# Norm passages of a three-block kernel: rows scaled first and turned by transposes, lower parts in one step, a new order of steps

## The reference, cut to what matters

```
def rmsnorm(x, g):                       # also rms_norm, rmsnorm_3
    return x * lax.rsqrt(jnp.mean(x * x, axis=-1, keepdims=True) + EPS) * g

# end of the first block
x = x + rmsnorm(mix, norm_post)          # mix = concat(...) @ w_out
# second block: begins and ends
h = rms_norm(x, norm_g);  proj = h @ w_in
...
x = x + y @ w_out
x = rms_norm(x, final_g)
# third block: begins
h = rmsnorm_3(h_res, ln_g) * (1.0 + scale[:, None]) + shift[:, None]
p = h @ w_in + b_in
```

## Time and profile before

| | us |
|---|---|
| median of three runs | 2825.24 |
| lowest, highest | 2823.49, 2826.43 |
| the profiled execution, device time | 2824.86 |
| its span on the profile page | 2823.0 |

### The profile page before, as it was taken

One profiled execution on the slowest core, in us unless ns is written; L12 is line 12 of the kernel. 1 busy time (PEld: TensorE's weight loads), 2 busy tenths in 40 slices (PEclk: granted clock), 3 DMA queues, 4 the chain that ended last, 5 costly groups with the idle time before them and its releaser, 6 DMA issues.

```text
span 2823.0 us, 38380 instructions
## 1 busy us (share of the span) xinstructions
PE 2793.6 (99%) x15512; PEld 2333.6 (83%) x15512; DVE 1409.7 (50%) x2509; ACT 1073.7 (38%) x1818; POOL 365.3 (13%) x627
## 2 busy tenths in 40 slices
PE   8999999999999999999999999999999999999998
PEld 7888777888899888888888889887777777788888
DVE  6686644436327544554554236335544453545534
ACT  5332234454226333322222236434443444333322
POOL 6457154100001000000000001000000000000011
PEclk9999999999999999999999999999999999999999
DMA  7567465324326444566664335542222223232423
GB/s 203 146 184 125 123 146 123 105 82 164 109 90 193 153 149 149 153 186 183 186 179 151 140 97 134 123 97 68 71 68 72 68 68 97 75 83 82 149 97 120
DMA packets 449153, 352.52 MB, mean 125 GB/s; under 512 B 73869, under 2 KB 404461, under 8 KB 444753
## 3 DMA queue, kind: packets, MB, share of 16 engines
q1 hardware_dynamic: 412818, 241.93, 30.6%
q0 software_dynamic: 36160, 108.14, 13.0%
HBM read 322.81 MB, written 22.81 MB: 122 GB/s over the span
## 4 chain that ended last, share of the span: by engine, by line
PE 95%; DVE 3%; DMA 1%; ACT 1%; issue 0%; POOL 0%; SPq 0%; DVEq 0%; ACTq 0%
PE bank L3615 57%; PE bank L3655 16%; PE bank L3625 4%; PE bank L3678 2%; PE bank L3573 2%; PE bank L2381 1%; PE bank L2432 1%; PE bank L2408 1%; PE bank L667 1%; DMA ring<-in_w_in 1%; PE bank L2502 1%; PE bank L2454 1%; PE bank L730 1%; DVE ring_parts L3768 1%; PE bank L694 0%; PE bank L663 0%
## 5 line engine op out<-in xcount | busy, mean ns | idle before, releaser
L3768 DVE TENSOR_TENSOR ring_parts<-ring,ring_hi 128x1024 fp32r<-128x1024 f32 x420 | 510.4, 1227 | 724.9 <-ACT ring_hi L3727 720.4
L3727 ACT ACTIVATE ring_hi<-ring 128x1024 fp32r<-128x1024 f32 (+1 forms) x424 | 441.3, 1051 | 599.9 <-DMA ring<-in_w_in 300.3
L3615 PE MATMUL bank<-A_parts,ring_hi 128*128 128x512 f32 x1552 | 618.2, 398 | 2.0 <-DVE ring_parts L3768 2.0
L3615 PE MATMUL bank<-A_parts,ring_parts 128*128 128x512 f32 x1552 | 605.6, 390 | 0.0
L3615 PE MATMUL bank<-X_parts,ring_hi 128*128 128x512 f32 x1360 | 529.6, 389 | 0.0
L3615 PE MATMUL bank<-B_parts,ring_hi 128*128 128x512 f32 x1224 | 478.8, 391 | 0.0
L3615 PEld LDWEIGHTS bank<-A_parts,ring_hi 128*128 128x128 f32 x1552 | 291.6, 188 | 66.7 <-issue 8.8
L3615 PEld LDWEIGHTS bank<-A_parts,ring_parts 128*128 128x128 f32 x1552 | 291.3, 188 | 62.5
L3615 PEld LDWEIGHTS bank<-X_parts,ring_hi 128*128 128x128 f32 x1360 | 255.6, 188 | 50.8
L3615 PE MATMUL bank<-B_parts,ring_parts 128*128 128x512 f32 x752 | 292.7, 389 | 0.0
L3615 PEld LDWEIGHTS bank<-B_parts,ring_hi 128*128 128x128 f32 x1224 | 230.0, 188 | 51.8 <-issue 5.1
(11 more groups left out here) (573 smaller groups left out, 3904.6 us busy)
## 6 DMA issues: line engine op xcount, KB each, us to landing
ring<-in_w_in SPq DMA_DIRECT2D x288, 512.0 KB, 3.8
ring<-in_w_out SPq DMA_DIRECT2D x96, 512.0 KB, 3.6
work<-in_w_ada POOLq DMA_DIRECT2D x96, 512.0 KB, 4.8
ring<-in_w_in SPq DMA_DIRECT2D x48, 256.0 KB, 3.8
ring<-in_w_mem_kv SPq DMA_DIRECT2D x16, 512.0 KB, 4.1
x_keep<-X POOLq DMA_DIRECT2D x8, 1024.0 KB, 4.8
X<-x_keep POOLq DMA_DIRECT2D x8, 1024.0 KB, 10.2
X<-in_x SPq DMA_DIRECT2D x4, 1024.0 KB, 10.9
```

What stands on the lines that cost most here:

```text
L3615: mm = nc.tensor.matmul(K.ps(st)[0:w + (t["beside"] or 0), 0:t["n"]], lhsT=wp[:, j, :], rhs=columns(ap, kk), start=first, stop=end)
L3727: nc.scalar.activation(slot_view[key](ring_hi), slot_view[key](ring), ACT.Copy).then_inc(s_hi, 1)
L3768: nc.vector.tensor_tensor(lo, slot_view[key](ring), slot_view[key](ring_hi), ALU.subtract).then_inc(s_lo, 1)
```

## The change

It does the following, and nothing outside the two passages:

- `d` makes the reciprocal and then scales the row tile itself by VectorE, in two halves of 1024 columns, into a buffer of its own (`K.scaled_rows`: in `K.work`, four buffers in passage one, two that are used in turn in passage two, where `d` of tiles 2 and 3 first waits that the tile two before is turned). In passage two both factors are applied in one instruction. PE waits for each half by itself.
- `T` turns the scaled rows by `nc.tensor.transpose` with the identity.
- In passage one `G` writes the rounded `h_hi` at once, and no longer waits for the store of `X`. `P` is, for each bank, four `scalar_tensor_tensor` of 128x128 that read the bank, multiply by the gain and subtract `h_hi`, giving `h_lo`; it waits for the store of `X`. Passage two keeps its `G` and `P`.
- `F` of passage two no longer waits for PE.
- Both orders in `LAST_COLUMNS` are new. In passage two F1, F2 and F3 now stand behind P31, and in passage one T00 ahead of W30.

```diff
--- before.py
+++ after.py
@@ -26,12 +26,12 @@
 
 
 LAST_COLUMNS = {
-    2: """W00 W10 W01 W11 E0 V0 M0 S0 R0 F0 W20 E1 V1 Q0 M1 W21 S1 m0 R1 s0 F1 W30 E2 d0 Q1 V2 M2 T00 S2 m1 R2 s1 F2 G00 W31
-          P00 a00 Q2 T01 d1 E3 m2 b00 G01 V3 T10 M3 P01 G10 T11 P10 s2 G11 d2 P11 T20 S3 a01 a10 T21 a11 R3 b01 F3 H00 b10 Q3
-          b11 m3 s3 G20 d3 P20 T30 G21 P21 T31 G30 H10 P30 G31 P31 H01 H11""",
-    3: """W00 W10 W01 W11 V0 E0 Z0 M0 S0 R0 m0 W20 V1 s0 E1 d0 Z1 M1 S1 R1 m1 T00 s1 d1 G00 T10 P00 T01 G10 W21 F0 G01 P10 W30
-          P01 V2 W31 E2 Z2 M2 S2 R2 m2 a00 T11 V3 s2 E3 d2 G11 M3 b00 T20 P11 T21 S3 a01 a10 b01 F1 F2 a11 H00 Z3 R3 b10 G20
-          m3 b11 s3 G21 d3 P20 T30 G30 P21 T31 P30 H10 G31 F3 P31 H01 H11""",
+    2: """W00 W10 W01 E0 M0 V0 S0 R0 W11 W20 E1 F0 M1 V1 S1 Q0 R1 F1 m0 s0 Q1 d0 m1 W21 E2 M2 T00 W30 V2 S2 R2 G00 s1 W31
+          F2 Q2 E3 T01 d1 P00 G01 V3 m2 T10 s2 M3 P01 T11 S3 a00 G10 d2 R3 b00 T20 a01 F3 a10 b01 P10 G11 Q3 P11 T21 m3 s3
+          H00 G20 b10 a11 d3 P20 T30 G21 T31 G30 b11 G31 P21 P30 H10 P31 H01 H11""",
+    3: """W00 W10 W01 V0 E0 Z0 M0 W11 S0 R0 m0 s0 V1 Z1 W20 d0 E1 T00 M1 W21 S1 R1 m1 s1 G00 d1 T10 P00 V2 G10 T01 E2 P10
+          G01 Z2 M2 W30 F0 S2 T11 W31 P01 a00 G11 R2 a01 V3 b00 E3 m2 P11 Z3 M3 s2 d2 a10 T20 S3 R3 G20 b01 b10 m3 T21 a11
+          H00 s3 P20 d3 T30 G21 G30 b11 P21 P30 T31 G31 H10 P31 F1 H01 F2 F3 H11""",
     None: """W00 W10 W01 W11 V0 E0 M0 S0 R0 F0 W20 V1 E1 M1 S1 R1 F1 W21 W30 V2 E2 M2 S2 R2 F2 W31 V3 E3 M3 S3 R3 F3"""}
 PROJ_BANKS = (0, 1, 2)
 PAIR_BANKS = (0, 1)
@@ -1430,16 +1430,26 @@
     x_keep = nc.dram_tensor("x_keep_2", (SEQ, D), F32).ap()
     s_keep = [K.sem(f"x_rows{tt}_kept_2") for tt in range(TT)]
     s_back = K.sem("x_back_2")
-    h_whole = K.X.rearrange("p t (k c) -> p t k c", c=P)
 
     def norm_parts(k4, tt):
         four = slice(4 * k4, 4 * k4 + 4)
-        return h_hi[:, four, tt * P:(tt + 1) * P], h_whole[:, tt, four, :], h_lo[:, tt, four, :]
-
-    def norm_gain_wait(act, tt):
-        act.wait_ge(s_par, K.par_count[2])
-        act.wait_ge(s_keep[tt], 16)
-    K.norm_parts[2], K.norm_gain_wait[2] = norm_parts, norm_gain_wait
+        hi = h_hi[:, four, tt * P:(tt + 1) * P]
+        return hi, hi, h_lo[:, tt, four, :]
+    K.norm_parts[2] = norm_parts
+    K.norm_gain_wait[2] = lambda act, tt: act.wait_ge(s_par, K.par_count[2])
+
+    def norm_lo(vec, src, k4):
+        tt = src[2]
+        if k4 == 0:
+            vec.wait_ge(s_keep[tt], 16)
+        vec.wait_ge(*bk.half_released(src, k4))
+        hi, _, lo = norm_parts(k4, tt)
+        for j in range(4):
+            kk = 4 * k4 + j
+            ins = nc.vector.scalar_tensor_tensor(lo[:, j, :], ps(src, k4)[:, j * P:(j + 1) * P], norm_g[:, kk:kk + 1], hi[:, j, :],
+                                                 ALU.mult, ALU.subtract)
+        ins.then_inc(bk.free_sem(src, k4), 1)
+    K.norm_lo[2] = norm_lo
     a = K.arena()
     v = a("b2_v", 2, TT, GLA_VD)
     r = a("b2_r", 2, 2, NC)
@@ -1828,7 +1838,6 @@
 
     def vec_final(vec, L, st):
         tt = st[2]
-        vec.wait_ge(*bk.filled(("norm", 3, tt), KT // 4 - 1))
         nc.vector.tensor_scalar(X[:, tt, :], X[:, tt, :], K.rstd_out[:, tt:tt + 1], None, ALU.mult).then_inc(K.x_done, 1)
 
     K.sq_junk[2] = K.hn[:, 1, :].rearrange("p (a c) -> p a c", c=NC)
@@ -3098,6 +3107,7 @@
         self.slot_src, self.slot_count, self.slot_used = {}, {"wo": 8}, {}
         self.const_loads, self.wait_gain, self.par_at = [], {}, 0
         self.sp_start, self.mix_parts, self.norm_parts, self.norm_gain_wait = [], {}, {}, {}
+        self.norm_lo = {}
         self.sq_junk, self.wo_releases = {}, {}
         self.act_wo_row, self.vec_wo_row, self.split_at = {}, {}, {}
         self.act_row_square, self.act_row_square_2, self.square_no, self.paired_tiles = {}, {}, {}, {}
@@ -3180,7 +3190,8 @@
         K.blocks, K.modulated = list(blocks), False
         K.par = K.sb("par", PAR)
         K.hn = K.work[:, 0:2 * D].rearrange("p (a d) -> p a d", d=D)
-        K.row_scale = {nxt: K.work[:, at:at + TT * P].rearrange("p (t c) -> p t c", c=P) for nxt, at in ((2, 6 * D), (3, 3 * D))}
+        K.scaled_rows = {2: lambda tt: K.work[:, tt * D:(tt + 1) * D],
+                         3: lambda tt: K.work[:, (3 * D, 6 * D + P)[tt % 2]:(3 * D, 6 * D + P)[tt % 2] + D]}
         K.sq = K.sb("square_sums", TT, SUMS)
         K.sq_2 = K.work[:, 4 * D:4 * D + TT * SUMS].rearrange("p (t n) -> p t n", n=SUMS)
         K.out_squared = K.work[:, 4 * D + TT * SUMS:4 * D + TT * SUMS + TT]
@@ -3275,11 +3286,15 @@
             nc.vector.reciprocal(r, r).then_inc(s_brstd, 1)
             vec.wait_ge(s_brstd, recip_no[st] + 1)
             if kind == "in_scale":
-                scale = K.row_scale[blk][:, tt, :]
-                if blk == 2:
-                    nc.vector.tensor_scalar(scale, K.ident[:, :], r, None, ALU.mult).then_inc(s_hn, 1)
-                else:
-                    nc.vector.tensor_scalar(scale, K.ident[:, :], r, out, ALU.mult, ALU.mult).then_inc(s_hn, 1)
+                if blk == 3 and tt >= 2:
+                    vec.wait_ge(*bk.filled(("norm", 3, tt - 2), KT // 4 - 1))
+                for half in range(2):
+                    cols = slice(half * D // 2, (half + 1) * D // 2)
+                    rows = K.scaled_rows[blk](tt)[:, cols]
+                    if blk == 2:
+                        nc.vector.tensor_scalar(rows, X[:, tt, cols], r, None, ALU.mult).then_inc(s_hn, 1)
+                    else:
+                        nc.vector.tensor_scalar(rows, X[:, tt, cols], r, out, ALU.mult, ALU.mult).then_inc(s_hn, 1)
 
 
         block_of = BLOCKS
@@ -3539,14 +3554,13 @@
                 if st[0] == "norm":
                     _, blk, tt, half = st
                     st = st[0:3]
-                    if half == 0:
-                        pe.wait_ge(s_hn, scaled_no["in_scale", blk, tt] + 1)
+                    pe.wait_ge(s_hn, 2 * scaled_no["in_scale", blk, tt] + half + 1)
+                    rows = K.scaled_rows[blk](tt)
                     for k4 in (2 * half, 2 * half + 1):
                         bk.take(pe, st, k4)
                         for j in range(4):
                             kk = 4 * k4 + j
-                            mm = nc.tensor.matmul(K.ps(st, k4)[:, j * P:(j + 1) * P], lhsT=X[:, tt, kk * P:(kk + 1) * P],
-                                                  rhs=K.row_scale[st[1]][:, tt, :], start=True, stop=True)
+                            mm = nc.tensor.transpose(K.ps(st, k4)[:, j * P:(j + 1) * P], rows[:, kk * P:(kk + 1) * P], K.ident[:, :])
                         mm.then_inc(bk.full_sem(st, k4), 1)
                 elif st[0] == "pair":
                     _, st, pair = st
@@ -3756,6 +3770,9 @@
                     if tt == 0 and h == 0:
                         K.wait_gain[blk](vec)
                     for k4 in (2 * h, 2 * h + 1):
+                        if blk in K.norm_lo:
+                            K.norm_lo[blk](vec, src, k4)
+                            continue
                         hi, whole, lo = K.norm_parts[blk](k4, tt)
                         vec.wait_ge(*bk.half_released(src, k4))
                         L(nc.vector.tensor_copy(hi, whole))
```

## The result

The changed kernel takes 2834.56 us (median of 7 runs, 2833.78 to 2835.74), the kernel before 2825.24 (7 runs, 2823.32 to 2828.09): ratio 1.0035, 95% interval 1.0026 to 1.0044. It is slower by 9.3 us; forecast were 6. The profiled execution took 2834.19 us, its span is 2832.4.

The account below looks back on a forecast made before the run. The prediction took both passages as ties between PE and the pair ACT and DVE, PE's savings kept only if P31 comes earlier. Its terms, 0.7 + 0.8 + 3.7 + 0.8 = +6.0 us, gave 2831, range 2822 to 2838.

Parts of the forecast that it names:

- Turns: PE time in both passages: transposes at 0.11 us instead of 0.23 save 14.7 us; bounds 0 and 14.7.
- Scaling: DVE time per row tile: 1.33 against 0.20 us in passage one, 1.46 against 0.25 in passage two.
- Lower parts: Subtractions of passage one on DVE: 1.05 us a bank against 1.06 before, neither gain nor loss; bounds -4 to +5 us.
- Passage one: P31 of passage one ends 0.7 us later and PE gives back all of its 7.4 us; bounds -0.5 to +4.
- the clock: PE's granted clock falls in idle times: +0.8 us in passage one, +0.8 behind passage two; bounds 0 and 3.2.
- Passage two: P31 comes 0.6 us earlier, PE stands idle some 8 us ahead of T20; bounds -1.2 and +1.5.
- The stores: Behind P31 of passage two: last store of x issued near 1749.8, 5.3 us later than before, landing at 1758.
- Behind the landing: From the last store's landing to the next tile 3.6 us: it starts at 1761.6, +3.7 us; bounds +0.2 and +8.3.
- the clock falls and the loads starve: Rival, chance 0.12: three clock falls at 1.6 us, stores landing at 1762.6, split slots late as well: +12 us, 2837.

Follow-up runs that it names:

- f_pool: The changed kernel with F0 to F3 of passage two on POOL, each as soon as its tile's halves are scaled: 2839.49 us, ratio 1.0053.
- turned_first: The changed kernel with the buffer `turned` moved to tile 0 of X, its writer waiting for that store alone: 2830.29 us, ratio 1.0020.
- f_ahead: The changed kernel with F1 to F3 of passage two ahead of P31 again: 2827.28 us, ratio 1.0008.

## Why the prediction came out as it did

The direction, the place of the loss and its mechanism (late stores, met by the weight loads, release the evacuation of `gates`) were right. The size was too small: the time of 2834.6 lies in the range, 3.6 us above the 2831 forecast, and it came that near in part by luck. Step by step:

- **Turns**: 0.11 us and a factor of two, as said; PE keeps nothing of it. Right. Timeline of PE and DVE, answering to the earlier trace rows:

```profile
881.87 1.91 PE L3563 MATMUL bank<-ident,work 128*128 128x128 f32 x16
```
```profile
860.46 1.42 DVE L3295 TENSOR_SCALAR work<-X,rstd 128x1024 f32<-128x1024 f32 x2
861.79 2.15 DVE L1449 SCALAR_TENSOR_TENSOR X_parts<-bank,par,B_parts 128x128 fp32r<-128x128 f32 x8
...
883.81 4.23 DVE L1449 SCALAR_TENSOR_TENSOR X_parts<-bank,par,B_parts 128x128 fp32r<-128x128 f32 x16 [0.51 <-ACT B_parts L3733]
```

- **Scaling**: two halves 1.42 us on DVE, so 1.3 to 1.4 a tile where I had 1.33. **Lower parts**: 16 scaled subtractions 4.23 us, 1.06 a bank, where I had 1.05. Both right.
- **Passage one**, +0.7 by P31 and +0.8 by the clock: between the two profiles both seem to be there. P31 ends 50.0 us behind the first W product (888.04 - 838.02), 49.4 before, and the passage is 1.57 us longer. Over twelve kernels neither stays. P31 ends at 49.4 to 49.5 us in all six of the old form and in four of the six of the new, at 50.0 and 50.1 in the other two, and the means of the passage are 0.05 us apart. The waits were 6.7 us, not 9.6. I took one profile of before for the typical one, and it was the fastest passage of its form: in the other five P31 ended in the same place, but PE began its 128 last products 0.9 to 1.1 us later (44.8 to 45.1 us behind the first W product, 44.0 in that one). The term was 1.5 us too high, give or take 0.6.
- **Passage two**, -0.6 at P31: it ended at 1745.63 (1745.7 forecast), the hole ahead of T20 was 7.9 us (8). Right. The clock fell in it to 0.50 and cost nothing there.
- **The stores**: issued last at 1749.53 (1749.8), landed at 1761.2. I took 1758, against the Trainium skill (DMA: Bandwidth & Descriptors, Issuing engines are not separate DMA queues), by which transfers interleave whoever issued them; by that alone I had 1762.6. The trace stands nearer to it. This step failed, the choice "nearer the end without loads, since the stores start first": SP issued loads from 1748.1 on, between the stores, and the DMA share was 1.11 and 1.07 from 1750 to 1762.
- **Behind the landing**: 3.6 us to the next tile, taken from rows at full clock. It was 4.9 (1761.2 to 1766.1), since 16 turns took 3.4 us at the lower level and not 1.7, and the split waited 1.25 us for its load. The first 48 products of the tile lost another 1.2 (12.2 us for 11.0). I had counted 0.8 for the clock and nothing for the load.

Together +3.7 and +0.8 should have been +9.4: 3.2 for the landing, 1.3 behind it, 0.4 of clock. (The three sum to 4.9.) The passage-one term, 1.5 too high, hid part of it: without it the sum would have been 4.5 us where 9.3 were measured. That is the luck. Of the rivals none came true as a whole; "the clock falls and the loads starve", 2837, described the end of passage two best. Open is why the clock in passage one fell in every profiled kernel but the one before, and how much of a cost below about 1 us is left in that passage.

## What to carry to other kernels

Before moving the instruction that releases a transfer, look at what the DMA engines do in the new place, and at every queue that shares them: here three stores, issued from 1746.6 to 1749.1 and not at 1732.3, 1733.7 and 1744.5, cost 8.7 us, and no place of the wait that I tried made them free. Where a passage is tied between two engines, faster work on one that is waiting anyway is worth nothing; take the time of the tie from several executions, not from one. And an idle gap may be made by the very steps one wants to put into it: find its releaser first.

## What the runs showed of the hardware

- In f_pool DVE stood while POOL scaled 128x2048 in float32: a cast of 0.42 us took 4.04 beside POOL's 5.5, and the same scaling takes DVE 1.28 us.
- SP's issue of a weight load, 0.4 us in the median and 1.3 at most before, took up to 5.3 us when stores of 3 MB were in flight (turned_first).
- The granted clock was 0.50 after an idle time of 7.9 us, and again after a wait of 1.9 us (f_ahead, 1750 to 1752), behind an earlier fall. Where nothing else held PE up that cost 1.2 to 1.5 us; in the hole ahead of T20, where PE waited for DVE anyway, nothing (H10 at 44.85 us with and without it).
